# A hybrid attention and short-convolution layer on one core: seven filler groups per attention unit and two more seven-product weight pairs

## The reference

```python
xn = rms_norm(x, norm_w)
h, gb, gc, q, k, v, g_conv, g_attn = jnp.split(xn @ w_in, SPLITS, axis=-1)
q, k = rms_norm(q per head), rms_norm(k per head)
u = gc * h
y_conv = gb * causal_conv(u, prefix, conv_w)          # 3 taps along time
y_attn = sink_attention(q, band(k), band(v), valid, sinks)
merged = jax.nn.sigmoid(g_conv) * y_conv + jax.nn.sigmoid(g_attn) * y_attn
x = x + merged @ w_out
xn = rms_norm(x, norm_ffn_w)
return x + (jax.nn.silu(xn @ w_gate) * (xn @ w_up)) @ w_down
```

## Time and profile before

| | us |
|---|---|
| median of 3 runs | 1664.97 (1664.53 to 1665.88) |
| the profiled execution | 1667.0 |
| its span, first to last instruction | 1664.9 |
| PE busy | 1645.3 |
| DVE busy | 1045.6 |
| POOL busy | 975.8 |
| ACT busy | 727.3 |

### The profile page before, as it was taken

The page is one execution under the profiler, slowest core; times in us unless marked ns, Lnnn a source line. Parts: engine busy times, 40 slices in busy tenths (PEclk is TensorE's granted clock), DMA queues, the critical chain, the costliest instruction groups (busy, mean ns, idle before and its releaser), DMA issues.

```text
span 1664.9 us, 28335 instructions
## 1 busy us (share of the span) xinstructions
PE 1645.3 (99%) x10751; PEld 1539.8 (92%) x10751; DVE 1045.6 (63%) x1597; ACT 727.3 (44%) x1631; POOL 975.8 (59%) x874
## 2 busy tenths in 40 slices
PE   7999999999999999999999999999999999999999
PEld 7999889898898999999888999999989999999998
DVE  6466665636666964475676667667686555555555
ACT  6333566636666323223155544544454333333331
POOL 3544533434556544443359878878888666666662
PEclk9999999999999999999999999999999999999999
DMA  5211111111110111114121232333333222222222
GB/s 180 48 39 38 48 33 32 32 42 33 32 33 29 39 52 51 52 40 164 53 89 64 90 114 90 102 115 97 94 127 108 82 77 86 80 77 88 86 80 77
DMA packets 125858, 120.44 MB, mean 72 GB/s; under 512 B 24218, under 2 KB 107454, under 8 KB 125728
## 3 DMA queue, kind: packets, MB, share of 16 engines
q1 hardware_dynamic: 120160, 115.89, 22.4%
q10 hardware_dynamic: 4896, 2.36, 0.5%
q0 software_dynamic: 672, 0.43, 0.1%
HBM read 113.34 MB, written 5.32 MB: 71 GB/s over the span
## 4 chain that ended last, share of the span: by engine, by line
PE 95%; DVE 3%; ACT 1%; issue 1%; DMA 0%; POOL 0%; SPq 0%; DVEq 0%; ACTq 0%
PE banks L2343 28%; PE banks L2002 23%; PE banks L2404 15%; PE banks L2231 13%; PE banks L2281 5%; PE banks L2166 2%; PE banks L2148 2%; PE banks L2025 2%; PE banks L2128 1%; PE banks L2038 1%; PE banks L2426 1%; PE banks L2015 0%; PE banks L2137 0%; PE banks L2320 0%; PE banks L2171 0%
## 5 line engine op out<-in xcount | busy, mean ns | idle before, releaser
L2002 PE MATMUL banks<-x_hi,w_hi 128*128 128x384 f32 x720 | 250.4, 348 | 0.0
L2343 PE MATMUL banks<-xc_hi,ring_a 128*128 128x256 f32 (+1 forms) x1200 | 247.9, 296 | 0.3 <-DVE u L1916 0.3
L2002 PE MATMUL banks<-x_hi,w_lo 128*128 128x384 f32 x720 | 241.4, 335 | 0.0
L2002 PE MATMUL banks<-x_lo,w_hi 128*128 128x384 f32 x720 | 241.3, 335 | 0.0
L845 POOL TENSOR_TENSOR ring_a<-raw_f,ring_a 128x512 fp32r<-128x512 f32 x133 | 191.1, 1449 | 22.7 <-ACT ring_a L1218 21.5
L2343 PEld LDWEIGHTS banks<-xc_hi,ring_a 128*128 128x128 f32 x1200 | 196.6, 190 | 1.0 <-DVE u L1916 0.6
L2343 PE MATMUL banks<-xc_lo,ring_a 128*128 128x256 f32 (+1 forms) x600 | 177.7, 296 | 0.0
L650 POOL TENSOR_TENSOR w_lo<-w_raw,w_hi 128x256 fp32r<-128x256 f32 x80 | 62.0, 808 | 182.1 <-ACT w_hi L898 182.1
L1938 DVE TENSOR_TENSOR X<-banks,X 128x512 f32<-128x512 f32 x190 | 123.3, 684 | 36.7 <-PE banks L2404 36.6
L2002 PEld LDWEIGHTS banks<-x_hi,w_hi 128*128 128x128 f32 x720 | 135.3, 188 | 4.4
L2002 PEld LDWEIGHTS banks<-x_lo,w_hi 128*128 128x128 f32 x720 | 135.5, 188 | 0.0
(11 more groups left out here) (324 smaller groups left out, 4227.6 us busy)
## 6 DMA issues: line engine op xcount, KB each, us to landing
raw_f<-in_w_gate SPq DMA_DIRECT2D x88, 256.0 KB, 3.1
raw_f<-in_w_up SPq DMA_DIRECT2D x88, 256.0 KB, 3.3
raw_f<-in_w_down SPq DMA_DIRECT2D x88, 256.0 KB, 2.8
w_raw<-in_w_in SPq DMA_DIRECT2D x64, 256.0 KB, 3.3
late_raw<-in_w_in SPq DMA_DIRECT2D x40, 256.0 KB, 3.0
X<-in_x_prompt SPq DMA_DIRECT2D x16, 512.0 KB, 7.2
w_raw<-in_w_out SPq DMA_DIRECT2D x16, 256.0 KB, 2.9
out_y_prompt<-X SPq DMA_DIRECT2D x16, 256.0 KB, 2.0
```

Of the source, the lines that this page charges most:

```text
L2002: mm = pe.matmul(banks[:, bank, 0:G], ws[slot][w][:, kt * P:(kt + 1) * P], xs[x][:, kt, g * G:(g + 1) * G], start=(kt == 0 and n == 0), st ...
L2343: mm = pe.matmul(banks[:, bank, 0:nb], ring(n)[:, w, k * P:(k + 1) * P], xc[x][:, X_OF_PROD[j], k, 0:nb], start=(start and k == 0 and z == 0),
```

## The change

- `LATE` gets two more pairs, (1, 3) and (1, 4), ahead of the ten: the two gate kinds of the slabs of i = 1. `TILES` lists the 16 slabs that are left for the attention stretch (20 before).
- PE goes through one list of (slab, token group, step) and does seven in each unit, four before the transposes and three behind them. A token group no longer ends where a unit ends: `end_slot` gives the unit in which it does, and ACT and DVE handle it there (`units_of`). 336 of the 384 groups lie inside the 48 units, the last two slabs (kinds 1 and 2) behind them. The bare stretch between i = 0 and i = 1 is gone; attention gates of i = 0 are now inside units.
- A slab's rounding on ACT stands between exponentials and scaling of the unit after the one in which the slab two before it ended (`slab_after`), and POOL's low parts move with it.
- The denominator is summed by a reduction over one operand.
- At the end of the attention stretch DVE's list holds three convolutions in place of six attention gates, with the sums of x between them. The first late pair is now gated, and the late pairs' waits are counted anew (`GATED`).
- In ACT's feed-forward `pair`, the copy of bank 1 is issued ahead of the ring roundings for c = 1, m = 0 too.
- The two buffers that the output weights take are swapped, because the number of slabs before them changes by four.

```diff
+TILES = [(0, jj, kind) for jj in range(2) for kind in range(4)] + [(0, jj, 4) for jj in range(2)] + \
+        [(1, jj, kind) for jj in range(2) for kind in range(3)]
+PER_SLOT = 7
+def end_slot(n, g):
+    return (24 * n + 8 * g + 7) // PER_SLOT
+def units_of(z):
+    return [(n, g) for n in range(len(TILES)) for g in range(3) if end_slot(n, g) == z and z < 2 * SLOTS]
+def slab_after(z):
+    return [n + 2 for n in range(len(TILES) - 2) if end_slot(n, 2) + 1 == z and z <= 2 * SLOTS]
...
-LATE = [(i, kind) for i in (2, 3) for kind in range(5)]
+LATE = [(1, 3), (1, 4)] + [(i, kind) for i in (2, 3) for kind in range(5)]
...
 ACT, exps
                 act.activation(soft[:, 5, 0:n], soft[:, 3, 0:n], ACT.Exp).then_inc(exp_done, 1)
+                if z:
+                    for m in slab_after(z):
+                        split_hi(Slab(PAIR_SLAB + m), "f", PAIR_FEAT + m - 2)
                 act.wait_ge(soft_done, 5 * z + 5)
...
 ACT, feed-forward pair
-                first = (p, c) == (0, 0)
+                first = (p, c) == (0, 0) or (c == 1 and m == 0)
...
 DVE, denominator
-                dve.tensor_tensor(soft[:, 6, 0:n], soft[:, 4, 0:n], soft[:, 5, 0:n], ALU.add).then_inc(soft_done, 1)
+                dve.tensor_reduce(soft[:, 6, 0:n], soft[:, 4:6, 0:n].rearrange("p k h -> p h k"), AX_X, ALU.add)\
+                    .then_inc(soft_done, 1)
...
 PE, attention units
+                        for k, group in enumerate(groups[z * PER_SLOT:(z + 1) * PER_SLOT]):
...
+                            if k == 4:
...
+                                if z:
+                                    s2(*before)
...
+                            feature_group(*group)
+                        if z:
+                            used = STEPS * i + t + 2 if u == 2 and following[0] < 2 else 1 if z == 1 else None
+                            s3(*before, used)
+            for k, group in enumerate(groups[2 * SLOTS * PER_SLOT:]):
+                if k == 0:
+                    s2(1, STEPS - 1, 2)
+                if k == 4:
+                    s3(1, STEPS - 1, 2)
+                feature_group(*group)
```

More of the change, by code:

```diff
@@ L183, in __init__ @@
         self.turn = first // 2 + (per // 2) * i
-        self.split = self.slot if isinstance(first, int) and first < OUT_SLAB else 1 - self.slot
-LATE = [(i, kind) for i in (2, 3) for kind in range(5)]
+        self.split = self.slot
+LATE = [(1, 3), (1, 4)] + [(i, kind) for i in (2, 3) for kind in range(5)]
+GATED = [sum(kind >= 3 for _, kind in LATE[:v]) for v in range(len(LATE))]
 LATE_OFF = (H_OFF, C_OFF, B_OFF, GC_OFF, GA_OFF)
@@ L522, in _ @@
                                 for h in range(2)])
[L524 to L532 removed]
+            for n, (i, jj, kind) in enumerate(TILES):
+                cols(Slab(PAIR_SLAB + n), w_in, LATE_OFF[kind] + (2 * i + jj) * P)
             for v, (i, kind) in enumerate(LATE):
@@ L1045, in unit @@
                     slot = (3 * jj + g) % 2
-                    if c > 3 or g > 1:
+                    if e > 1:
                         act.wait_ge(sg_used, e - 1)
-                    gate = S_g if i == 1 and kind == 4 else S
+                    gate = S_g if n == len(TILES) - 1 else S
                     act.activation(gate[:, slot, :], bank, ACT.Tanh, scale=0.5).then_inc(bank_free[b], 1)
@@ L1662, in late_pair @@
                     dve.wait_ge(conv_step, 36 + 6 * (i - 2) + 3)
-                if kind == 3:
+                if v == 0:
+                    for b in range(3):
+                        dve.wait_ge(bank_free[b], LATE_FEAT)
+                elif kind == 3:
                     dve.wait_ge(lc11_done, v)
@@ L2174, in _, with feature_group @@
             pe.wait_ge(masks_done, 21)
+            def feature_group(n, g, kt):
+                bank = LAST_BANKS[g] if n == len(TILES) - 1 else g
+                if kt == 0:
+                    if g == 0:
+                        pe.wait_ge(w_lo, PAIR_SLAB + n + 1)
+                    pe.wait_ge(bank_free[bank], PAIR_FEAT + n)
+                for z, (w, x) in enumerate(PASSES):
+                    mm = pe.matmul(banks[:, bank, 0:G], ws[n % 2][w][:, kt * P:(kt + 1) * P],
+                                   xs[x][:, kt, g * G:(g + 1) * G],
+                                   start=(kt == 0 and z == 0), stop=(kt == KT - 1 and z == 2))
+                if kt == KT - 1:
+                    mm.then_inc(gemm_ready, 1)
@@ L2175, in _ @@
+            groups = [(n, g, kt) for n in range(len(TILES)) for g in range(NG) for kt in range(KT)]
             for i in range(2):
                 for t in range(STEPS):
-                    f = PAIR_FEAT + 10 * i + t
                     for u in range(3):
-                        before = None if 3 * t + u == 0 else ((t, u - 1) if u else (t - 1, 2))
+                        z = SLOTS * i + 3 * t + u
+                        bi, bz = divmod(z - 1, SLOTS)
+                        before = (bi, bz // 3, bz % 3)
```

229 lines of the change are left out of this document (104 added, 125 removed).

## The result

| | before | changed |
|---|---|---|
| median, us | 1664.97 (1664.53 to 1666.2, 5 runs) | 1672.94 (1671.71 to 1673.89, 5 runs) |
| span of the profiled execution | 1664.9 | 1671.5 |

The ratio is 1.004, 95% interval 1.0029 to 1.0051. The prediction had 1660.7 with a range to 1664.8.

What follows compares the result with a forecast made beforehand. PE, busy for 99% of the span, was taken as the bound. Late pairs -5.3, copy -2.8 and waits +3.8 gave -4.3, so 1664.97 - 4.3 = 1660.7 us, with a range from just under the whole gain (1657.1) to 1664.8.

Steps and rivals of the forecast that it cites:

- Step 1: Attention stretch and late stage: four filler slabs (49.9 us) leave, two late pairs (44.6 us) come in; net -5.3 us.
- Step 3: In attention units, three groups leave DVE's copy 0.2 us of cover ahead of probability x value: waits sum to +3.8 us.
- step 5: Attention units: ACT's weight rounding (1.06 us) between exponentials and scaling fits in ACT's idle time; counted at nothing.
- Step 4: Attention units: the one-operand denominator takes 0.2 us; worth nothing directly, only 0.5 us used at the gates.
- Step 2: Feed-forward part: the copy `prod` ahead of two weight roundings removes PE's gaps, 2.4 and 0.4 us; -2.8 us.
- Step 6: Start of the late stage: DVE does convolutions and multiplications in place of attention gates; bounds 0 and +3 us, taken as 0.
- the slower one: Rival, attention units: three groups don't cover the copy, every four-head unit waits; 1672.8 us at 0.5 each; chance 0.06.
- The rival with half of the copies late: Attention units: DVE operations blocking against POOL make half the copies late; 1665.5 us, from 1663.5 to 1667; chance 0.15.

Runs made afterwards that it cites:

- the swapped version: Changed kernel with gatings and B multiplications later, rounding first, sums of x early, plus DVE's low part of x ahead of the last addition into `t4`: 1662.98 us, ratio 0.9983.

## Why the prediction was wrong

| step | predicted | shown |
|---|---|---|
| 1, two more late pairs | -5.3 | -5.3 in PE work (late +45.95, of it 1.4 a wait) |
| 2, the copy | -2.8 | -2.2 between the profiled executions, -0.7 to -1 where before has no slow clock |
| 3, waits ahead of probability x value and scores of unit 1 | +3.8 | +10.6 |
| 5, rounding between exponentials and scaling | 0 | in the row above: 3.6 of its waits go when it is undone |
| 6, start of the late stage | 0, bound +3 | +1.4 |
| the clock in the attention stretch | not thought of | some +3 |

**Step 1 held.** The late pairs run at their pace behind the first products. What PE gains is what the arithmetic says.

**Step 3 failed, and it decides the sign.** It summed the waits ahead of probability x value to +3.8, and they came to +10.6. It looked for gates in the *first* unit of a step: 12, 27, 30 and 33. It gave units 31 and 34 1.0 for both, and they waited 0.77 each; 22 and 43 got 1.2 each and waited 1.5 and 1.4; unit 1 with its scores got 1.0 and took 1.0. All of that is near. Missing are the gates in the *second* unit, 28 and 31: the waits in 29 and 32 are 2.5 and 2.6, 5.1 us together, with nothing against them in the sum. The prediction took each cause for itself: gates by DVE's list, the rounding by ACT's idle time (step 5), POOL's operations beside the convolution alone. In units 28 and 31 the three meet. Units 34 and 35 have the same order on DVE without the rounding and without POOL, and no wait; the sums of x early take 1.9 us from each of the two waits with the order on DVE as it was; the gates later take both waits whole with POOL's and ACT's lists as they were, 6.6 us with the 0.77 of units 31 and 34. In the kernel before attention gates stood in the bare stretches, where they could not meet a unit's softmax. Unit 8 was said to have room as a short sample unit, and waited 0.90 (0.42 in another execution of the same code), of it 0.3 for `cache_kT`: its three fillers are the same as anyone's cover, and a short list of its own doesn't help against the convolution ahead of the copy.

**Step 5 failed.** Its argument was that ACT idles there. ACT does, and 0.7 of the 1.07 us is hidden by it; but behind the scaling stands the tanh that DVE waits for, and 0.4 reaches DVE where a gate follows. The rest comes by POOL, whose low parts follow the rounding and whose sums of x follow those: they run beside the gate and the small operations behind it in units 28, 29, 31 and 32, and beside the convolution in 21 and 42 (its last four operations and the first copy of tails take 2.85 and 0.70 in unit 21, against 2.16 and 0.15 with the rounding first). Undoing it took 0.60 and 1.36 from units 29 and 32 and 0.5 each from 22 and 43. The part at the convolution stood in a rival, at 2.8 at most; the part at the gates stood nowhere.

**Step 4 was right:** under 0.17 us in all units, and worth nothing; the 0.5 that it was to give back at the gates isn't seen either, as the waits with the add are the same to 0.02 us.

**Step 2 had the mechanism and a size 0.6 too large.** It found no next wait, by setting DVE's adds against PE's 24 matmuls; PE stood for `gate` after 12. The second pass gave the 0.4 that it was to give. Three waits appear later, for DVE's `gate`, for `prod` and for `X`: the gaps between PE's starts there are 0.93, 0.53 and 0.80 where the pace is 0.12, 0.12 and 0.21, 1.8 us more. The 1.2 us of slow clock behind the old gap, which went too, wasn't in the sum and made up for most of that. The two errors had opposite signs, and that they nearly cancel is luck. The sum also said that no term depends on the 2 us between the profiled execution and the median. This one does: the profiled execution had the half-clock piece and the median one, by its time, had not, so counted from 1664.97 the copy is worth about 1, of which the times show 0.7.

**Step 6 took the good end of its own bounds.** DVE and POOL at the start of the late stage, which answer to the 2.55 of a low part in the earlier trace rows:

```profile
524.43 6.77 DVE L1539 TENSOR_TENSOR t_full<-t_full,x_lo 128x2304 f32<-128x2304 f32 x2
531.13 3.65 DVE L1544 TENSOR_TENSOR x_lo<-t_full,x_hi 128x2304 fp32r<-128x2304 f32 x1
...
523.65 5.14 POOL L848 TENSOR_TENSOR late_ring<-late_sums,late_ring 128x512 fp32r<-128x512 f32 x2 [10.20 <-ACT late_ring L1108]
528.76 10.75 POOL L848 TENSOR_TENSOR late_ring<-late_raw,late_ring 128x512 fp32r<-128x512 f32 x3
```

The sums took 3.4 us each and the low part 3.65 beside POOL's low parts of the weights, where before it took 2.55, and PE waited:

```profile
523.90 6.38 PE banks L2263 x48
...
530.32 0.82 issue
531.13 3.66 DVE x_lo L1544
...
534.84 225.24 PE banks L2263 x1698
```

This cause is read from the rows; the one run on it only moved the wait.

Of the rivals, the slower one came nearest in time (1672.8) but not in mechanism: it wanted every four-head unit to wait, and in the changed kernel nine waits of 48 cost 12.2 us, while ordinary units show no wait, as worked out. The rival with half of the copies late named DVE operations that block beside POOL. That is 1.9 us of each of the two long waits, but in two units and not in 16.

**What stays open.** Whether a given wait of 2.5 us brings the slow clock. The same code does it in one execution and not in the next (before: 33 of 89 had it, 56 not). In the profiles, by the gaps between PE's starts, the half clock came behind 2.78 and 2.85 (changed kernel, and about the same with the add), 2.64 (transposes earlier), 2.79 (copy put back, unit 29) and the 2.53 of before. It did not come behind 2.81 (copy put back, unit 32), the 2.50 for `prod` there, the 2.54 for POOL's low parts in the swapped version, nor behind any gap up to 2.26 in these parts. No run moved a wait alone without its surroundings. Nor did a run move `cache_kT` or the rounding without POOL's low parts, so the split of the long waits into 0.3, 0.4 and the rest is read from rows. The 0.4 us of the stretch is unplaced.

## What to carry to other kernels

When work is spread evenly over units so that PE's cover shrinks, write down for each unit what all engines do there, and look for the units in which several small costs meet; priced one by one, each here was hidden in most units. Follow each waiting instruction into the *next* unit and ask what stands behind it. A gate that waits for a tanh belongs one unit later, where its input is ready (here worth 0.5% of the time by itself), and moving an operation on one engine moves what follows it on another: POOL's low parts came with ACT's rounding. A small gain on the bounding engine is quickly eaten by two waits of 2.5 us and the clock behind them. With DVE's gates and multiplications a unit later and the rounding put back ahead, the change is a gain, 0.9978 (0.9968 to 0.9987).

## What the runs showed of the hardware

- TensorE fell to 1.2 GHz for 3.4 us around the end of gaps of 2.5 to 2.9 us between PE's starts, in the middle of otherwise dense work. It cost 1.1 to 1.6 us each time, and not every such gap brought it: the same kernel had it in 33 of 89 executions.
- A DVE operation on one column with two SBUF operands took 0.16 us alone and up to 1.33 us beside POOL's; on 2304 columns the low part took 2.55 and 3.65. In these rows the smallest operations suffer most in proportion.
- The tail of one and the same code lay at 878.9 to 879.2 us in most profiles and at 880.2 and 880.3 in two (gates later, rounding first), by a wait for DVE's `gate` of 1.3 in place of 0.7. A difference of 1 us in a single profile isn't an effect by itself.
